# A chunked delta-rule scan: per-head 64x64 state, its two products on quarters of the array, state-free products moved ahead, state update in two vector operations

## The reference, cut to what matters

```python
def step(st, inp):
    r_t, w_t, k_t, v_t, a_t, b_t = inp
    sa = jnp.einsum('bhvk,bhk->bhv', st, a_t)
    st = st * w_t[:, :, None, :] + sa[..., None] * b_t[:, :, None, :] + v_t[..., None] * k_t[:, :, None, :]
    y = jnp.einsum('bhvk,bhk->bhv', st, r_t)
    return st, y
...
s0 = jnp.zeros((bsz, nh, n, n), jnp.float32)
_, ys = lax.scan(step, s0, xs)
```

## Time and profile before

| | us |
|---|---|
| median of 3 runs | 3843.76 (3840.67 to 3855.43) |
| the profiled execution | 3830.29 |
| its span | 3828.5 |
| the scan in it | from 2332.6 to 2541.4 |
| its mixed stretches | from 2371 to 2507.5 |
| its tail | from 2507.5 to 2541.4 |

### The profile page before, as it was taken

The page is one execution under the profiler, slowest core; times in us unless marked ns, Lnnn a source line. Parts: engine busy times, 40 slices in busy tenths (PEclk is TensorE's granted clock), DMA queues, the critical chain, the costliest instruction groups (busy, mean ns, idle before and its releaser), DMA issues. The chain is left out here.

```text
span 3828.5 us, 54923 instructions
## 1 busy us (share of the span) xinstructions
PE 3604.5 (94%) x22742; PEld 2749.3 (72%) x22742; DVE 2058.1 (54%) x2358; ACT 1207.3 (32%) x1716; POOL 1875.7 (49%) x1064
## 2 busy tenths in 40 slices
PE   5999899889899999899999998989999899999998
PEld 5888544578788744578887777876577788878877
DVE  4443577553444466563466734545542788874242
ACT  3234344431223344432123422324401444441020
POOL 1443266544255266544355643303633699973433
PEclk9999899999999999999999999998999899999999
DMA  5112200025211200022221230020043122224112
GB/s 185 39 39 68 70 1 1 26 90 201 74 39 62 54 1 1 26 100 89 83 72 50 75 95 24 4 100 1 1 137 115 63 82 93 83 104 167 60 50 72
DMA packets 101935, 258.02 MB, mean 67 GB/s; under 512 B 29232, under 2 KB 38576, under 8 KB 100800
## 3 DMA queue, kind: packets, MB, share of 16 engines
q1 hardware_dynamic: 83008, 215.42, 16.5%
q10 hardware_dynamic: 18688, 39.20, 3.1%
HBM read 200.02 MB, written 54.56 MB: 66 GB/s over the span
## 5 line engine op out<-in xcount | busy, mean ns | idle before, releaser
L1846 PE MATMUL acc<-h_hi,weights_hi 128*128 128x512 f32 (+1 forms) x928 | 347.3, 374 | 7.7 <-DVE h_lo L2015 5.3
L1091 DVE TENSOR_REDUCE part_max<-aux 128x1 f32<-128x428 f32 (+5 forms) x468 | 252.8, 581 | 179.7 <-PE aux L932 128.2
L1847 PE MATMUL acc<-h_lo,weights_hi 128*128 128x512 f32 (+1 forms) x928 | 338.6, 365 | 0.0
L1848 PE MATMUL acc<-h_hi,weights_lo 128*128 128x512 f32 (+1 forms) x928 | 338.4, 365 | 0.0
L2553 PE MATMUL acc<-h_hi,weights_hi 128*128 128x512 f32 x672 | 271.9, 405 | 0.0
L2555 PE MATMUL acc<-h_hi,weights_lo 128*128 128x512 f32 x672 | 263.2, 392 | 0.0
L2554 PE MATMUL acc<-h_lo,weights_hi 128*128 128x512 f32 x672 | 262.9, 391 | 0.0
L2029 DVE RECIPROCAL arena<-arena 128x512 f32<-128x512 f32 (+1 forms) x48 | 141.7, 2953 | 223.3 <-ACT arena L1992 223.3
L1053 ACT ACTIVATE probs<-acc 128x1024 f32<-128x1024 f32 (+1 forms) x168 | 168.4, 1003 | 252.6 <-PE acc L967 252.0
L978 PE MATMUL acc<-probs,v_tok 128*64 128x512 f32 (+3 forms) x864 | 222.4, 595 | 2.2 <-DVE inverse L1111 2.2
L3721 PE MATMUL acc<-operand_hi,weights_hi 128*128 128x512 f32 x504 | 197.3, 391 | 10.8 <-POOL weights_lo L3455 10.8
(11 more groups left out here) (525 smaller groups left out, 9167.4 us busy)
## 6 DMA issues: line engine op xcount, KB each, us to landing
weights<-in_w_in SPq DMA_DIRECT2D x44, 512.0 KB, 3.5
arena<-in_w_mod SPq DMA_DIRECT2D x6, 2048.0 KB, 8.8
weights<-in_w_up SPq DMA_DIRECT2D x24, 512.0 KB, 4.2
weights<-in_w_out SPq DMA_DIRECT2D x22, 512.0 KB, 4.9
weight_sums<-feed_forward_spill SPq DMA_DIRECT2D x22, 512.0 KB, 4.6
xT<-in_w_up SPq DMA_DIRECT2D x20, 512.0 KB, 4.2
weights<-in_w_mod SPq DMA_DIRECT2D x4, 2048.0 KB, 26.5
mixer_gates<-arena SPq DMA_DIRECT2D x32, 256.0 KB, 2.0
```

Of the source, the lines that this page charges most:

```text
L1091: nc.vector.tensor_reduce(part_max[:, b % 2, j, hh, i:i + 1], max_tile(m)[:, hh, 0:cw], AX_X, ALU.max, negate=True).then_inc(max_done, 1)
L1846: nc.tensor.matmul(out, w_hi[:, b, k, :], hi[:, k, cols], start=(k == 0), stop=False)
L1847: nc.tensor.matmul(out, w_hi[:, b, k, :], lo[:, k, cols], start=False, stop=False)
L1848: return nc.tensor.matmul(out, w_lo[:, b, k, :], hi[:, k, cols], start=False, stop=(k == KD - 1))
```

## The change

The state tile becomes `[128, 4, 64]`, in which each head has a 64x64 block on its own half of the partitions. X-state and Y-state are now eight 64x64 matmuls each, with head `2p` on rows and columns 0 to 63 of the array and head `2p + 1` on rows and columns 64 to 127. In `s` = 0, X-k and then Y-k come first, and X-state last; `state_ready` is waited for only ahead of X-state. In `s` = 1, S-k is followed by Y-state alone. Two new semaphores, `x_begun` and `y_begun`, make PE wait for its own X-k ahead of X-state and for its own Y-k ahead of Y-state. The wait for `y_copied` goes to `s` = 0 with Y-k. DVE updates the state in two operations: one addition on 128x256 and one multiplication on 128x256. The list `order` is the same.

```diff
-        u_sb, state = (tail[:, n_masks + c:n_masks + c + 512].rearrange("p (h n) -> p h n", n=n) for c, n in ((0, CHUNK), (512, P)))
+        u_sb, state = (tail[:, n_masks + c:n_masks + c + w].rearrange("p (h n) -> p h n", n=CHUNK) for c, w in ((0, 512), (512, pairs * HD)))
...
                     if s == 0:
-                        pe.wait_ge(state_ready, n + 1)
...
                         for p, odd in both:
-                            nc.tensor.matmul(ps_x[halves[odd], p, :], pair(a_in, p), state[:, p, odd * HD:(odd + 1) * HD],
-                                             start=(p == 0), stop=False, skip_group_check=True)
+                            mm = nc.tensor.matmul(ps_x[halves[odd], p, :], by_k[rows, b, 1, odd * pairs + p, :], tok[rows, b, 2, column(p, odd)],
+                                                  start=(p == 0), stop=False, skip_group_check=True)
+                        mm.then_inc(x_begun, 1)
+                        if n >= 2:
+                            pe.wait_ge(y_copied, n - 1)
                         for p, odd in both:
-                            mm = nc.tensor.matmul(ps_x[halves[odd], p, :], by_k[rows, b, 1, odd * pairs + p, :], tok[rows, b, 2, column(p, odd)],
+                            mm = nc.tensor.matmul(ps_y[n % 2][halves[odd], p, :], tok[rows, b, 2, column(p, odd)], by_k[rows, b, 0, odd * pairs + p, :],
+                                                  start=(p == 0), stop=False, skip_group_check=True)
+                        mm.then_inc(y_begun, 1)
+                        pe.wait_ge(x_begun, n + 1)
+                        pe.wait_ge(state_ready, n + 1)
+                        for p, odd in both:
+                            mm = nc.tensor.matmul(ps_x[halves[odd], p, :], pair(a_in, p)[halves[odd]], state[halves[odd], p, :],
                                                   start=False, stop=True, skip_group_check=True)
                         mm.then_inc(x_ready, 1)
                     elif s == 1:
-                        wait_used(pe, t, BY_K)
...
-                        if n >= 2:
-                            pe.wait_ge(y_copied, n - 1)
-                        for p in range(pairs):
-                            nc.tensor.matmul(ps_y[n % 2][:, p, :], state[:, p, :], pair(z, p), start=(p == 0), stop=False, skip_group_check=True)
+                        pe.wait_ge(y_begun, n + 1)
                         for p, odd in both:
-                            nc.tensor.matmul(ps_y[n % 2][halves[odd], p, :], tok[rows, b, 2, column(p, odd)], by_k[rows, b, 0, odd * pairs + p, :],
+                            nc.tensor.matmul(ps_y[n % 2][halves[odd], p, :], state[halves[odd], p, :], pair(z, p)[halves[odd]],
                                              start=False, stop=False, skip_group_check=True)
...
-                        for odd in range(2):
-                            block = state[halves[odd], :, odd * HD:(odd + 1) * HD]
-                            step.done(tt(block, block, ps_s[halves[odd]], ALU.add))
-                        tt(state, state, end_decay[:, :, n:n + 1].to_broadcast([P, R_TILES, P]), ALU.mult).then_inc(state_ready, 1)
+                        step.done(tt(state, state, ps_s, ALU.add))
+                        tt(state, state, end_decay[:, :, n:n + 1].to_broadcast([P, R_TILES, HD]), ALU.mult).then_inc(state_ready, 1)
```

More of the change, by code:

```diff
@@ L3012, in rwkv_scan @@
         sum_begun, own = pg.sem("sum_begun"), pg.sem("dve_step")
+        x_begun, y_begun = pg.sem("x_begun"), pg.sem("y_begun")
         halves = (slice(0, CHUNK), slice(CHUNK, P))
```

## The result

| | before | after |
|---|---|---|
| median, us (7 runs each) | 3843.76 (3829.01 to 3860.09) | 3823.04 (3820.19 to 3824.82) |
| the profiled execution | 3830.29 | 3824.74 |
| its span | 3828.5 | 3822.9 |

The ratio is 0.9946, with a 95% interval from 0.9925 to 0.9967. The kernel is faster by 20.7 us, 0.54%. The median was forecast at 3824.9.

What follows compares the result with a forecast made beforehand. The prediction took the scan to be bound by PE's issue of blocks, with a short wait for the state in the tail. Tail -7.0, mixed stretches -12.7 and added wait +0.8 took 3843.8 to 3824.9 us, range 3814 to 3835.

Steps and rivals of the forecast that it cites:

- The tail: Scan's last four chunks: blocks 0.88 us shorter each, waits for the state gone, last update shorter; 7.0 us saved.
- The added wait: PE's wait for its own X-k ahead of X-state: 0.05 us a chunk, 0.8 us in all, at most 2.7.
- The mixed stretches: Scan's three pairs of tiles, four chunks each: only blocks count, 4.23 us saved a pair, 12.7 us in all.
- Does other work come up late?: Check in the mixed stretches whether PE would wait for DVE's copy of L3086's result: slack 0.45 us, copies not binding yet.
- The block prices: Start-to-start times of PE's blocks in the scan: 0.46 us ahead of a 64x64 block, 0.62 ahead of another shape.
- The half-gain rival: Mixed stretches: copies by DVE or ACT bind, so 12.7 us becomes 6.4, total -12.6, time 3831; 11 in 100.
- Exclusion: X-state and Y-state: quarters writing one PSUM bank take turns, 0.92 us instead of 0.46, time 3840; 8 in 100.
- The clock: Tail and next stage's first 14.5 us run at 1.2 GHz, costing 31.5 us, net +12.6, time 3856; 3 in 100.
- The sum: Whole kernel: -7.0 - 12.7 + 0.8 = -18.9 us, taken from the median 3843.8, giving 3824.9.

Runs made afterwards that it cites:

- the compact state alone: Changed kernel with the old order of products (X-state ahead of X-k, Y-state ahead of Y-k), compact state and two-operation update kept: 3829.87 us, 0.9971 of before.
- the dense run: Changed kernel plus 1,024 passes of 64 moving columns, then 1,024 of 128, without waits, behind PE's last scan instruction: 3882.41 us.
- the two later comparisons: Changed kernel rerun unchanged against the kernel before on the same chip: 3824.88 against 3841.08 us, and 3822.49 against 3844.51 us.

## Why the prediction came out as it did

The median was forecast at 3824.9 and is 3823.0, inside the range of 3814 to 3835. The gain of 0.54% lies just on the side of "faster by over 0.5%", which had 38 in 100; its interval reaches to both sides of that line. That the number fits is partly luck, as the steps show.

**The tail: right.** 7.0 us were forecast, and 6.96 were measured. The step from 3.34 to 2.46 in each chunk, the wait of 0.44 that goes and is replaced by none, and the 0.43 of DVE's multiplication (0.42) all came as worked out.

**The added wait: too dear.** 0.8 us was taken for `x_begun`. X-state starts 0.30 to 0.46 us after Y-k in the later chunks of the tail (the first passes of a block can overlap the last of the one before), and 0.54 at its start, where the state is ready only at 2507.87:

```profile
2507.45 0.55 PEld L3111 LDWEIGHTS acc<-by_k,token_major 64*64 64x64 f32 x16
2507.99 0.54 PEld L3117 LDWEIGHTS aux<-arena 64*64 64x64 f32 x15
```

The lower bound, nothing, holds wherever Y-k stands between. What the wait costs bare is 0.28, as the compact state alone showed; the upper bound of 0.17 was no bound for that case.

**The mixed stretches: wrong by half.** 12.7 us were forecast and 6.2 came. The failed step is the one headed "Does other work come up late?". It looked for what could hold PE back among copies and concluded "Copies do not bind yet", which is true, and did not ask whether PE's own instructions arrive in time. The block prices themselves were right: with each block of a pair at its shortest of the three pairs, a pair takes 45.96 us in both traces of before and 41.6 to 41.7 in those of after, 4.3 less (4.2 forecast). Above these sums the mixed stretches lose 1.4 and 3.8 us in before and 9.3, 10.5 and 8.1 in after. In the mean that is 6.7 us more, which is what is missing of the 12.7. The "idle" of the table grows by only 4.5, since a stop shows shorter than it is: the first cut shown has 0.66 us of idle time, and its next pass starts 0.80 late.

Measured from one pair's first X-k to the next pair's, the pairs take 45.1, 43.5 and 44.1 in the first trace of after, where 42.2 was forecast. A pair has 1,360 passes (1,328 before; the transposes, unlike the other matmuls, are one pass each), since four 128-row matmuls a chunk became eight. With PE's semaphore instructions that is 10.9 portions of 256, against 10.6 before. An estimate: at 4.0 us a portion it makes 43.5 us of supply beside blocks of 41.7; before, it was 42.5 beside blocks of 46.0, and PE seldom caught up. At 3.75 us, which the dense run also shows, it would be 40.8, so the mean over a pair doesn't decide it alone: PE is held where quick blocks stand together and a packet comes late. So the change made the blocks shorter than the supply of their instructions, and the bound moved.

**The half-gain rival: right in size, wrong in cause.** It had said 6.4 and named copies by DVE or ACT. The runs show supply instead.

**Exclusion: refuted.** X-state to S-k takes 0.42 (2520.49 to 2520.91 above), where taking turns was to give 0.92, and this is the rule in the traces of after; where such a block stands longer, it is cut by an idle time of the kind above. The Trainium skill (TensorEngine Tiling (Array Packing), Gotcha 1: PSUM Pressure) has different row tiles unable to access one PSUM bank simultaneously. Here two row halves wrote one bank, each its own 64 partitions, at the full rate of two quarters; for this arrangement the measurement decides against the rule.

**The clock: refuted.** The granted clock is 1.00 in the tail in all three traces of after. In the 15 us behind it, it is 1.00, 0.96 and 0.92, and 1.00 and 0.94 in the two of before. So it does fall there in some executions, but in both kernels, and nowhere near the 41.5 us that the rival counted.

**The sum: right by a second error.** The scan gave 12.0 instead of 18.9. The medians differ by 20.7, and in the two later comparisons by 16.2 and 22.0. Of this 4 to 10 us don't lie in the scan. In the traces, the rest of the span, whose code is the same, varies by some 10 us within one kernel (3619.7 and 3630.3 before; 3623.8 to 3630.1 after).

The difference goes with the granted clock. Of 50 later executions of before the mean clock of the whole execution is known: 0.961 to 0.973, 0.9678 in the mean, and 0.001 less goes with 2.9 us more (correlation -0.95). The 22 executions of after have 0.968 to 0.972, 0.9700 in the mean. At that clock before's line gives 3836.3 us, and after's mean time is 3823.5: 12.8 less at the same clock, within a microsecond of the scan's 12.0. The other 6.5 of the 19.3 us between the mean times go with before's lower clock. In the traces the clock is 1.00 in the scan's mixed stretches and tail, so the lower values lie elsewhere; whether the change has any part in them stays open.

So the scan's error of 6.9 us and the difference of the clock, which the prediction did not have, nearly cancelled. Before's profiled execution was 13.5 us below its median and after's 1.7 above. The prediction took the sum from the median, since nothing tied the 13.5 to the scan; that was an assumption. Against the profiled execution the step would have given 3811.4, and it was 3824.7.

## What to carry to other kernels

Price a row of small matmuls twice, by the blocks' distances and by the number of their instructions; where quick and slow blocks alternate, now the one holds and now the other, and the row takes longer than its blocks alone say (here 43.5 to 45.1 us for a pair with 41.7 of blocks and an estimated 43.5 of supply). Cutting one matmul into two smaller ones raises the second. Here a wait for one's own product cost nothing where one independent block stood between, and 0.28 us where none did. Where two kernels' times differ by more than their traces explain, set the times against the granted clock of each execution. And once a wait is gone, try again whether what was put in to fill it (here the fillers) still earns its time.

## What the runs showed of the hardware

- PE got its instructions in portions of 256 (128 passes and 16 KB, one packet of the instruction queue). In the dense run a portion came every 4.02 or 3.75 us, whether its passes took 15 ns (1.95 us for 128) or 27 ns (3.48 us) each; with packets of 0.88 to 0.93 us instead of 1.12 to 1.46 the supply kept up with 27 ns. The lack shows as idle time ended by "issue", at multiples of 256 instructions from each other, also in the middle of a block.
- In the dense run PE was busy for 4.18 of 8.00 us at the full clock; in the next 7.80 us the granted clock was 0.56 in the mean, most of it at the 1.2 GHz level:

```profile
2539.75:2547.75 8.00, 4.18 (x256) 3.91 (x256) 0.00 (x0) 0.00 (x0) 0.00 (x0) 1.00 0.02 4
2547.75:2555.55 7.80, 6.72 (x256) 6.34 (x256) 0.00 (x0) 0.00 (x0) 0.00 (x0) 0.56 0.02 4
```

It took no time there: at the lower clock the same 128 passes filled the idle time, and the portions came 3.75 and 4.02 us apart.

- Two quarters on the diagonal of the array, with both row halves writing one bank, take 0.42 to 0.46 us for 16 passes (X-state and Y-state). U, whose two row halves write two banks, takes 0.61 us ahead of another shape (2522.91 to 2523.52 in after), so 0.45 by the price of 0.16 for the change.
